# Wide down stage of a SwiGLU decoder layer: three pieces of side work issued at other units

## What is computed

```python
def swiglu(h, w_gate, w_up, w_down):
    return (jax.nn.silu(h @ w_gate) * (h @ w_up)) @ w_down

x = x + 0.5 * swiglu(rmsnorm(x, ffn1_norm[l]), ffn1_w_gate[l], ffn1_w_up[l], ffn1_w_down[l])
...                                   # mixers, cross attention
x = x + 0.5 * swiglu(rmsnorm(x, ffn2_norm[l]), ffn2_w_gate[l], ffn2_w_up[l], ffn2_w_down[l])
return rmsnorm(x, final_norm)
```

## Time and profile before

| what | value |
|---|---|
| median of 3 executions | 1992.12 us (1989.2 to 1993.02) |
| profiled execution, its own time | 1990.86 us |
| its span, first to last instruction | 1989.1 us |
| TensorE (PE) busy | 1961.5 us, 99% of the span |
| weight loads of TensorE (PEld) busy | 1616.5 us, 81% |
| DVE busy | 1528.9 us, 77% |
| ACT busy | 1062.3 us, 53% |
| mean granted TensorE clock | 0.998 of full speed |

### The profile page before, as it was taken

The page is one execution under the profiler, slowest core; times in us unless marked ns, Lnnn a source line. Parts: engine busy times, 40 slices in busy tenths (PEclk is TensorE's granted clock), DMA queues, the critical chain, the costliest instruction groups (busy, mean ns, idle before and its releaser), DMA issues. The chain is left out here.

```text
span 1989.1 us, 27433 instructions
## 1 busy us (share of the span) xinstructions
PE 1961.5 (99%) x10022; PEld 1616.5 (81%) x10022; DVE 1528.9 (77%) x1906; ACT 1062.3 (53%) x1305; POOL 13.6 (1%) x19
## 2 busy tenths in 40 slices
PE   9999999999999999999999999999999999999998
PEld 7888888887787888878777888888888888877886
DVE  7899899988875555776657675689998899888644
ACT  6555555555554444455555564555555555554443
POOL 0000000000000000000002000000000000000000
PEclk9999999999999999999999999999999999999999
DMA  8566666666665557655433465566556656655764
GB/s 299 190 203 190 200 209 189 191 209 234 213 213 183 190 169 214 188 187 163 138 121 115 158 203 169 158 228 205 191 191 209 196 194 210 199 198 196 243 192 148
DMA packets 148546, 382.69 MB, mean 192 GB/s; under 512 B 13424, under 2 KB 19824, under 8 KB 148080
## 3 DMA queue, kind: packets, MB, share of 16 engines
q1 hardware_dynamic: 146368, 378.70, 59.3%
q10 hardware_dynamic: 2096, 2.87, 0.4%
HBM read 377.33 MB, written 4.19 MB: 192 GB/s over the span
## 5 line engine op out<-in xcount | busy, mean ns | idle before, releaser
L584 ACT ACTIVATE w_hi<-w_raw 128x1024 fp32r<-128x1024 f32 x694 | 725.8, 1056 | 685.4 <-PE psum L1853 330.6
L1094 DVE TENSOR_TENSOR w_lo<-w_raw,w_hi 128x1024 fp32r<-128x1024 f32 x694 | 835.8, 1221 | 316.9 <-ACT w_hi L584 314.5
L1889 PE MATMUL psum<-w_hi,xT_hi 128*128 128x512 f32 x920 | 360.3, 392 | 0.0
L1889 PE MATMUL psum<-w_hi,xT_lo 128*128 128x512 f32 x920 | 358.6, 390 | 0.0
L1889 PE MATMUL psum<-w_lo,xT_hi 128*128 128x512 f32 x920 | 358.4, 390 | 0.0
L1853 PE MATMUL psum<-w_hi,xT_hi 128*128 128x512 f32 (+1 forms) x544 | 213.0, 392 | 2.6 <-DVE w_lo L1211 2.3
L1853 PE MATMUL psum<-w_hi,xT_lo 128*128 128x512 f32 (+1 forms) x544 | 209.5, 385 | 0.0
L1853 PE MATMUL psum<-w_lo,xT_hi 128*128 128x512 f32 (+1 forms) x544 | 209.3, 385 | 0.0
L1889 PEld LDWEIGHTS psum<-w_hi,xT_lo 128*128 128x128 f32 x920 | 172.8, 188 | 36.0
L1889 PEld LDWEIGHTS psum<-w_lo,xT_hi 128*128 128x128 f32 x920 | 172.9, 188 | 35.2
L1889 PEld LDWEIGHTS psum<-w_hi,xT_hi 128*128 128x128 f32 x920 | 172.8, 188 | 35.0
(11 more groups left out here) (319 smaller groups left out, 2510.6 us busy)
## 6 DMA issues: line engine op xcount, KB each, us to landing
w_raw<-in_gu SPq DMA_DIRECT2D x351, 512.0 KB, 4.3
w_raw<-in_d SPq DMA_DIRECT2D x176, 512.0 KB, 4.5
w_raw<-in_w_in SPq DMA_DIRECT2D x88, 512.0 KB, 4.3
w_raw<-in_w_out SPq DMA_DIRECT2D x32, 512.0 KB, 3.8
w_raw<-in_cw SPq DMA_DIRECT2D x8, 512.0 KB, 4.4
w_raw<-in_wk SPq DMA_DIRECT2D x8, 512.0 KB, 3.9
w_raw<-in_wq SPq DMA_DIRECT2D x8, 512.0 KB, 3.6
w_raw<-in_wv SPq DMA_DIRECT2D x8, 512.0 KB, 3.6
```

Source lines behind the costliest of these rows:

```text
L584: nc.scalar.activation(w_hi[:, slot], w_raw[:, slot], ACT.Copy).then_inc(w_hi_ready, 1)
L1094: nc.vector.tensor_tensor(w_lo[:, slot], w_raw[:, slot], w_hi[:, slot].bitcast(F32), ALU.subtract)\
L1889: mm = nc.tensor.matmul(psum[:, bank, :], act_t, w, start=(first and n == 0), stop=(last and n == 2))
```

## The change

Three pieces of side work are issued at other positions. No instruction is added or removed.

- The last gated products are transposed at position 1 instead of 3, and their hi and lo parts are taken at position 2 instead of 4.
- The lo part of the token sums of a pair is made four positions ahead of it instead of three.
- Batch 1 of x is transposed behind unit 8 of group n = 2 instead of unit 5, and taken at unit 9 instead of 6.

```diff
@@ ffn_down on ACT
-                    if p == 4:
+                    if p == 2:
                         take(b_h + FF_CHUNKS - 1, 0, ffT_hi, KF - 4)
...
-                            if n == 2 and k in (4, 6):
-                                i = int(k == 6)
+                            if n == 2 and k in (4, 9):
+                                i = int(k == 9)
                                 take(b_x + i, 0, xT_hi, 4 * i, s_x + 4 * i)
@@ ffn_down on DVE
-                    if p == 4:
+                    if p == 2:
                         take(b_h + FF_CHUNKS - 1, 0, ffT_lo, KF - 4, ffT_hi, KF - 4)
...
-                    if p + 3 in DOWN_AT:
-                        i = DOWN_AT.index(p + 3)
+                    if p + 4 in DOWN_AT:
+                        i = DOWN_AT.index(p + 4)
                         token_lo(i % 3, S_FFN * nth + NP + i + 1)
...
-                            if n == 2 and k in (4, 6):
-                                i = int(k == 6)
+                            if n == 2 and k in (4, 9):
+                                i = int(k == 9)
                                 take(b_x + i, 0, xT_lo, 4 * i, xT_hi, 4 * i, s_x + 4 * i)
@@ ffn_down on TensorE
-                    if p == 3:
+                    if p == 1:
                         pe.wait_ge(h_ready, base_c + FF_CHUNKS)
                         batch(b_h + FF_CHUNKS - 1, 0, lambda j, t: comb[:, 2 * t + 1, j * P:(j + 1) * P])
...
-                            if n == 2 and k in (3, 5):
-                                i = int(k == 5)
+                            if n == 2 and k in (3, 8):
+                                i = int(k == 8)
                                 pe.wait_ge(x_ready, xr + 2)
                                 batch(b_x + i, 0, x_tiles(i))
```

## The result

The changed kernel takes 1976.92 us (median of 4 runs, 1975.94 to 1977.94), beside 1991.87 us for the kernel before (4 runs, 1989.2 to 1993.02; the three of the section on the time before and one more). The ratio is 0.9927, 95% interval 0.991 to 0.9944: 14.95 us faster. A second comparison on another occasion gave 1976.37 against 1989.21 us (0.9936, 0.9922 to 0.9949): 12.84 us. The forecast was 13.4 us and a time of 1978.7 us in a range of 1976.5 to 1983.5, so the measured time lies inside, 0.4 us from the lower edge. The profiled executions, 1990.86 before and 1977.94 us after, are 12.9 us apart.

A forecast was written before the change was run, and what follows sets the result against it. TensorE, busy 99% of the span, was taken as the bound, so only its idle time counted. 4.45 + 5.04 + 2.20 + 1.7 = 13.4 us off 1992.12 gave 1978.7 us, range 1976.5 to 1983.5.

The forecast's parts named there:

- The bound: Whole kernel: TensorE is busy 99% of the span, so only a change to its few microseconds of standing still can show.
- Down stages, 9.5 us: Pairs of both down stages: all waits with their restarts go, 4.45 us in the second stage and 5.04 in the first.
- Batch 1 of x, 2.2 and 1.7 us: First half step: TensorE's 2.20 us wait for batch 1's lo part goes, and 1.7 us of half clock after it.
- the sum: Whole kernel: 4.45 + 5.04 + 2.20 + 1.7 = 13.4 us gained, with nothing subtracted since no instruction is added.
- the rival that leaves the 1.7 us out: Batch 1 of x: half clock is chance, absent from the typical execution; only 11.7 us gained, 1980.4 us; chance 0.20.
- The margins: Down-stage pairs: moved DVE pieces end 2.3 us early or more at first pairs; at later pairs `t_lo` is 2.4 early.
- What is late next is `t_lo`, and it is 2.4 us early: Later down-stage pairs: `t_lo` ends 14.61 us after the first pair's start, and TensorE needs it at 17.00.
- `t_lo` or a load takes the place of `s_lo`: Rival, down stages: the ten later waits stay, 1984.9 us; 1.9 us load wait against 2.4 us margin; chance 0.07.
- The slower rival: Down stages: TensorE waits at position 1 for gated products, margin 0.68 us; at 10 us lateness 1997 us; chance 0.03.
- DVE durations: Ahead of the first pair: take, `s_lo`, `t_lo` and second `w_lo` durations added up, ending at 1754.48, 1755.16, 1756.92 and 1758.14.

The follow-up runs named there:

- The two edits alone: Kernel before with both down-stage edits (transposes and take earlier, lo part of token sums four positions ahead), batch 1 of x left behind unit 5: 1979.89 us, ratio 0.9945.
- each of the two edits alone: Kernel before with only the lo part of the token sums four positions ahead: 1982.81 us; with only transposes at position 1 and take at 2: 1986.4 us.
- batch 1 alone: Kernel before with only batch 1 of x moved behind unit 8 and taken at unit 9: 1986.77 us, ratio 0.9979.
- `s_lo` alone: Kernel before with only the lo part of the token sums made four positions ahead instead of three: 1982.81 us, ratio 0.9962.
- half loads and three repetitions: Changed kernel, wide down stages loading half of each weight unit, `w_lo` of each pair's first unit computed three more times: 1998.07 us.
- three repetitions: Changed kernel with `w_lo` of each pair's first unit computed three more times in the down stages, whole loads: 2012.85 us, ratio 1.0116.
- half loads: Changed kernel with only the first half of each weight unit loaded in the wide down stages, nothing added on DVE: 1977.75 us.
- two repetitions: Changed kernel with `w_lo` of each pair's first unit computed two more times in the down stages, whole loads: 1996.62 us, ratio 1.0042.

## Why the prediction was right

**The bound.** Right: only TensorE's idle time counted, and the change removed the three rows of waits and no work.

**Down stages, 9.5 us.** Shown. The two edits alone gave 10.6 us with 9.5 inside the interval, the pairs stand 15.64 us apart in all five profiles that have both with whole loads and nothing added on DVE, and each of the two edits alone gave its part. The wait of the very first pair is not the same in every execution: 1.52 us in the kernel before and 2.18 us with batch 1 alone, whose down stages are the same. The cause was the order of DVE, not its load: `s_lo` alone brought 7.7 us with the same instructions.

**Batch 1 of x, 2.2 and 1.7 us.** The wait of 2.2 us was right and is gone in every profile with the batch at unit 8 or 6. The 1.7 us of half clock were in the sum in full; they followed the same idle time in two of four profiles, and the mean clock is lowered in 19 of 38 executions of the kernel before. An average over executions is nearer to 0.9, and the sum nearer to 12.6 us than to 13.4. The forecast gave the rival that leaves the 1.7 us out a chance of 0.20; the record has it about as often as not, so here the forecast was too sure of one trace. The two comparisons gave 14.95 and 12.84; both intervals hold 12.6 and 13.4, and the runs do not tell between them. That the first lies 1.5 us above the sum has no row that explains it, and the second does not show it. With a term in the sum that about half of the executions have, and runs of one kernel that differ by 3 us and more, how near the time came to 1978.7 is in part luck. The Trainium skill ("TensorE: Matmul & The Clock Gate", Part 1) says that the point of a change of the clock varies from run to run. On this the traces agree: in the kernel before, the eight transposes right behind the idle time take 1.87 us already, and with the down stages alone they take 1.06 us and the first slow matmul starts 1.1 us after their start:

```profile
613.52 1.06 PE L1876 MATMUL psum<-ident,x 128*128 128x128 f32 x8 [2.04 <-DVE xT_lo L1130]
...
614.65 0.62 PE L1853 MATMUL psum<-w_lo,ffT_hi 128*128 128x512 f32 x1
```

**The margins.** The step that was mis-sized, though it did not change the outcome, is "What is late next is `t_lo`, and it is 2.4 us early". The place of `t_lo` was right: it ended 14.30 us after the first pair's start against 14.61 in the forecast. But a margin of one instruction is not the room of a loop, and two things were missing. A delay that comes in every period also spends DVE's idle time, of which a period has about 2.1 us: with half loads and three repetitions DVE is full. And with whole loads only 0.8 to 1.0 us can be spent, since a late `w_lo` starts the load into its slot late, and the next weight sums wait for that load. For the same reason the rival "`t_lo` or a load takes the place of `s_lo`" was not excluded by 1.9 being less than 2.4, as I wrote. It did not come. Ahead of the second pair `w_lo` of the second unit starts 3.40 us behind that of the first (1763.73 - 1760.33), where it was 3.32 before (1773.77 less 1772.09 - 0.42 - 1.22), so the loads' release moved by 0.1 us only; that this is why is argued, not shown. In the first down stage, where loads of the memory stand in the same queue, the changed kernel already shows 2.6 us of waits for loads that TensorE does not feel.

**The slower rival.** Its margin of 0.68 us at position 1 was sized rightly: at position 0 TensorE waits 2.10 us per stage.

**DVE durations.** Rows of consecutive DVE instructions overlap by 0.08 us, so my sums over four of them were 0.3 us too long, on the safe side.

## What to carry to other kernels

Read what an in-order engine does just ahead of the instruction that is waited for, and ask of each piece when it is really due: here the piece needed first stood last, and moving 0.68 us of work past 3 us of other work was worth about 6 us. When a margin is worked out in a loop, ask two more things. How much idle time has the engine in a whole period? And what does the late instruction release: follow the buffer that it frees and the load that fills it. Here one instruction's margin was 2.7 us, DVE's idle time per period about 2.1, and with the loop through the loads 0.8 to 1.0 were left. And a clock that fell behind an idle time in one trace need not fall in the next: count the idle time in full and the half clock as a chance, which the mean clocks of several executions can put a number on.

## What was not expected of the hardware

Between 2.0 and 2.6 us of idle time on TensorE, the length does not tell whether 1.2 GHz follows. All figures here are the idle times that the timeline gives in brackets. 2.04 us were followed by it in two profiles and not in two. In the trace with three repetitions 2.19 and 2.60 us were followed by it, while 2.34 us, one pair earlier, were not; the clock column of the two stretches behind the idle times of 2.34 and 2.19 us:

```profile
1787.00:1799.00 12.00, 11.89 (x51) 9.61 (x52) 10.71 (x14) 3.82 (x4) 0.00 (x0) 1.00 0.75 251
1805.40:1811.00 5.60, 5.54 (x17) 4.29 (x18) 4.98 (x4) 0.94 (x1) 0.00 (x0) 0.70 0.58 196
```

Near the start of the program 2.48 us in the changed kernel stayed at full clock, and 2.08 us in the one with half loads did not. The three longest, 2.99, 3.23 and 3.53 us, all in the trace with three repetitions, were each followed by it. No idle time under 2.0 us was in any profile; the longest of them is 1.99 us, in the trace with two repetitions.
